# The last five column chunks of an input projection, computed by seven block products of 4 matmuls in place of 16 full ones

## Chip, cores and metric

The kernel runs on one core of a Trainium2 chip. The metric is the device time of one execution in microseconds (us), lower is better. Before the change three runs took 1416.8, 1419.84 and 1420.33 us, a median of 1419.84 us.

## What is computed

Two layers of a hybrid backbone for two groups of 128 tokens (a context group and a latent group), D_MODEL 1024, all in float32. Cut to the part that the change touches, a layer is:

```python
h  = x * (1 + scale1) + shift1                      # 2 groups x 128 tokens x 1024
(aq, ak, av, ao, gates, bq, bk, bv, cf_f, cf_b, cq, ci, cg,
 ga, gb, gc) = split(h @ w_in_l + b_in_l)           # w_in_l: 1024 x 9232
a_out, b_out, c_out = mlstm(...), attention(...), hgrn2(...)
y = (sigmoid(ga) * (a_out @ w_branch[0]) + sigmoid(gb) * (b_out @ w_branch[1])
     + sigmoid(gc) * (c_out @ w_branch[2])) @ w_out
x = layer_norm(ALPHA * x + gate1 * y)
y = hier_moe(x * (1 + scale2) + shift2)             # 16 experts
x = layer_norm(ALPHA * x + gate2 * y)
```

`ga`, `gb` and `gc` are 1024 wide each: they are the last six blocks of 512 columns of the projection. Keys, values and final states are outputs too.

## The kernel before

**Tiling.** The projection of a layer is cut into 18 chunks (`N_IN`) of 512 columns. A chunk's weights are one slot of 128 partitions x 4096 floats (2 MB), streamed into a ring of three slots (`ring`) by the SyncE queue; a slot is asked for again as soon as its last reader has counted up `slot_used`. The activations lie turned in `hT` (features on partitions, 8 blocks of 128, by 256 tokens). For a chunk TensorE runs, for each of the two groups of tokens, 8 matmuls with a 128x128 block of `hT` as stationary operand and 512 weight columns moving (line 974; a float32 matmul leaves two records in the trace, so 16 matmuls are "x32"). Three early chunks are computed turned, with 256 moving columns (line 970). VectorE reads each group's 512 sums from its own PSUM bank (`PJ`, `PJ + 1`), adds the bias and writes `ch` (line 1662).

**Order.** The program is written by hand in "quarters": quarter `q` of a layer belongs to chunk `q // 4`; quarters 0 and 1 of a chunk are group 0, quarters 2 and 3 group 1. Each engine's loop over quarters first emits the rounds of the recurrences that are set to that quarter (`in_order`), and then its share of the chunk. The rounds (`H_ROUNDS`, `T_ROUNDS`) are chains that go from TensorE to the other engines and back: each round waits on TensorE until the round before it is done on all engines. In the last chunks of a layer the rounds of the neighbourhood attention are left. Those of one head parity of the latent group are: scores (`na_scores`, quarters 58 and 63, lines 878 and 881 on TensorE, lines 1606 to 1617 on VectorE, with one ScalarE Exp, line 1289, in the middle), probabilities (`na_probs`, quarters 60 and 65, line 727) and output (`na_out`, quarters 62 and 67, lines 890 and 892).

**Between the chunks.** After some chunks a slot with modulation weights is multiplied by 8 narrow matmuls of 512 columns (`mod_products`, line 744, bank `MODS`), which VectorE adds to `rows` (line 1668): in layer 0 after chunks 13, 14, 15 and 16 among others, in layer 1 after chunk 14 only, of the last five.

**Sigmoids.** Chunks 12 to 17 are `ga`, `gb` and `gc`. Their sigmoid is ScalarE Exp (line 1334), GpSimd +1 and minimum (line 1970, `sig_plus`), ScalarE Ln and Exp (lines 1336 and 1337), for one group of one chunk at a time, in the one buffer `sig`.

**End of the stage.** At quarter 68 (`TURN_AT`) the branches' outputs are transposed (line 911) and the modulation rows summed (lines 961 and 777); after the last chunk the branch products follow (line 998), which wait for `rows_copied`, `mod_ready` and `br_ready`. The loads of the norm's weights and the gates into `hbuf` stand in the SyncE queue after the load of the first branch slot (`norm_and_gates`).

## Time and profile before

| what | value |
|---|---|
| median of three runs | 1419.84 us |
| profiled execution, its span (the rows and sums below are of this one) | 1419.9 us |
| TensorE (PE) busy | 1355.3 us, 95% |
| weight loads (PEld) busy | 744.6 us, 52% |
| VectorE (DVE) busy | 507.2 us, 36% |
| ScalarE (ACT) busy | 222.8 us, 16% |
| GpSimd (POOL) busy | 149.8 us, 11% |
| DMA | 376.28 MB, mean 265 GB/s |
| input projection, branches and output projection of layer 0 and of layer 1 | end near 460 and 1140 us |

Busy time is the time in which at least one instruction of the engine ran; TensorE's matmuls overlap, and their ends are modelled. Which engine sets the time has to be read stage by stage: the span holds two layers, each with an input projection (chunks 0 to 17), branch and output projections, and 16 experts.

### The profile page before, as it was taken

How to read it: one execution, taken by the hardware profiler on the slowest of the kernel's cores; microseconds unless marked ns; L12 is line 12 of the kernel's file. 1: busy time of each engine (PE TensorE's matmuls, PEld its weight loads, DVE VectorE, ACT ScalarE, POOL GpSimd, SP SyncE). 2: the span in 40 equal slices, each digit the busy share in tenths (PEclk: the TensorE clock that was granted, in tenths of full speed). 3: DMA queues.
4: the chain of work that ended last, by engine and by line, in shares of the span. 5: the costliest groups of instructions: out<-in, count | busy, mean ns of one | idle time of the engine just before them, and what ended most of it. 6: DMA issues, size and time to landing. Idle time of an engine off the chain costs nothing. (4 is left out here: it accounts for less than half of the span.)

```text
span 1419.9 us, 17185 instructions
## 1 busy us (share of the span) xinstructions
PE 1355.3 (95%) x6796; PEld 744.6 (52%) x6796; DVE 507.2 (36%) x972; ACT 222.8 (16%) x430; POOL 149.8 (11%) x131
## 2 busy tenths in 40 slices
PE   5999999999999999999989999999999999999994
PEld 2675545444545555555537655554554465555552
DVE  1224454433134422332252345452313343232324
ACT  0011221222201111111110213112230111011110
POOL 0002441022100000000001044402120000000000
PEclk9899999999999999999999999999999999999998
DMA  9655644556455899999993526343426729999993
GB/s 382 244 209 193 235 192 156 237 192 252 163 202 229 332 393 399 399 413 414 411 369 140 216 110 230 134 147 135 192 85 265 296 74 393 398 414 393 413 412 137
DMA packets 44488, 376.28 MB, mean 265 GB/s; under 512 B 13066, under 2 KB 17290, under 8 KB 21644
## 3 DMA queue, kind: packets, MB, share of 16 engines
q1 hardware_dynamic: 36000, 372.18, 65.3%
q10 hardware_dynamic: 8428, 3.29, 0.9%
q8 instruction: 40, 0.66, 0.2%
q14 instruction: 20, 0.16, 0.0%
HBM read 371.11 MB, written 4.33 MB: 264 GB/s over the span
## 5 line engine op out<-in xcount | busy, mean ns | idle before, releaser
L974 PE MATMUL psum<-ring,hT 128*128 128x512 f32 x960 | 431.5, 598 | 5.6 <-ACT hT L1187 2.2
L974 PEld LDWEIGHTS psum<-ring,hT 128*128 128x128 f32 x960 | 177.4, 191 | 206.0 <-issue 197.8
L1094 PE MATMUL psum<-ring,tbuf 128*64 128x256 f32 x1920 | 216.0, 380 | 3.5 <-DMA ring<-in_stream 3.5
L1094 PEld LDWEIGHTS psum<-ring,tbuf 128*64 128x64 f32 x1920 | 136.0, 137 | 96.8 <-issue 20.3
L1133 PE MATMUL psum<-ring,tbuf 128*64 128x512 f32 x512 | 116.9, 598 | 1.9 <-ACT tbuf L1382 1.9
L1812 DVE TENSOR_SCALAR tbuf<-tbuf 128x256 f32<-128x256 f32 x32 | 9.4, 294 | 243.8 <-ACT tbuf L1372 243.8
L1662 DVE TENSOR_TENSOR ch<-psum,bias_ring 128x512 f32<-128x512 f32 x56 | 38.6, 690 | 140.9 <-PE psum L974 140.9
L970 PE MATMUL psum<-hT,ring 128*128 128x256 f32 x384 | 85.4, 380 | 0.0
L998 PE MATMUL psum<-ring,tbuf 128*128 128x512 f32 x192 | 82.9, 593 | 0.0
L970 PEld LDWEIGHTS psum<-hT,ring 128*128 128x128 f32 x384 | 72.5, 190 | 13.0 <-issue 3.7
L1970 POOL TENSOR_SCALAR ldata<-ldata 128x512 f32<-128x512 f32 x24 | 46.1, 1920 | 253.2 <-ACT ldata L1334 241.5
L1078 PE MATMUL psum<-tbuf,ch 128*128 128x128 f32 x512 | 65.0, 281 | 6.8 <-DVE tbuf L1807 5.0
L1133 PEld LDWEIGHTS psum<-ring,tbuf 128*64 128x64 f32 x512 | 34.1, 136 | 69.8 <-issue 58.5
L1101 PE MATMUL psum<-tbuf 64*128 64x512 f32 x256 | 67.4, 626 | 1.4 <-ACTq L540 0.7
L1078 PEld LDWEIGHTS psum<-tbuf,ch 128*128 128x128 f32 x512 | 59.4, 191 | 15.5 <-issue 8.5
L998 PEld LDWEIGHTS psum<-ring,tbuf 128*128 128x128 f32 x192 | 36.3, 190 | 45.1 <-issue 45.0
L1012 PE MATMUL psum<-ring,hT 128*128 128x512 f32 x128 | 55.8, 594 | 1.4 <-ACT hT L1344 1.4
L1813 DVE RECIPROCAL tbuf<-tbuf 128x256 f32<-128x256 f32 x32 | 56.1, 1753 | 1.1
L355 POOL TENSOR_TENSOR hbuf<-hbuf 128x512 f32<-128x512 f32 x28 | 46.0, 1644 | 90.5 <-PE psum L797 90.5
L797 PEld LDWEIGHTS psum<-hbuf 128*128 128x128 f32 x256 | 34.4, 192 | 17.6 <-issue 12.9
L1385 ACT ACTIVATE tbuf<-psum 128x512 f32<-128x512 f32 x32 | 19.1, 597 | 154.7 <-PE psum L1133 154.7
L1807 DVE COPY tbuf<-psum 128x512 f32<-128x512 f32 x32 | 22.1, 691 | 51.4 <-PE psum L1078 51.4
(279 smaller groups left out, 1161.5 us busy)
## 6 DMA issues: line engine op xcount, KB each, us to landing
ring<-in_stream SPq DMA_DIRECT2D x154, 2048.0 KB, 9.7
ch<-in_stream SPq DMA_DIRECT2D x8, 2048.0 KB, 13.7
bias_ring<-in_b_in SPq DMA_DIRECT2D x30, 256.0 KB, 8.2
ldata<-in_ldata SPq DMA_DIRECT2D x2, 2329.0 KB, 19.8
tbuf<-in_stream SPq DMA_DIRECT2D x2, 2048.0 KB, 14.4
hbuf<-in_ln SPq DMA_DIRECT2D x4, 1024.0 KB, 10.7
hbuf<-in_stream SPq DMA_DIRECT2D x1, 2048.0 KB, 8.6
hbuf<-row_mem SPq DMA_DIRECT2D x2, 1024.0 KB, 4.7
```

Of the source, the lines that this page charges most:

```text
L355: return engine.tensor_tensor(v, v, other.unsqueeze(3).to_broadcast([P, 2, W // (2 * half), half]), ALU.mult)
L970: mm = pe.matmul(psum[:, PJ + g, part * G * P:(part + 1) * G * P], w[:, k, (2 * g + part) * P:(2 * g + part + 1) * P], hT[:, k, :], start= ...
L974: mm = pe.matmul(bank(PJ + g), hT[:, k, g * P:(g + 1) * P], w[:, k, :], start=(k == 0), stop=(k == KT - 1))
L998: mm = pe.matmul(bank(BR_BANK[g] + hf), brT[:, b % 2, k, g * P:(g + 1) * P], w[:, k, hf * W:(hf + 1) * W], start=(k == 0), stop=(k == BT - 1))
L1012: mm = pe.matmul(bank(2 * hf + g), hT[:, k, g * P:(g + 1) * P], w[:, k, :], start=(k == 0), stop=(k == KT - 1))
L1078: mm = pe.matmul(psum[:, at, j * P:(j + 1) * P], h2tok[:, g, (4 * part + j) * P:(4 * part + j + 1) * P], e_pick[:, g, :], start=(g == 0), ...
L1094: mm = pe.matmul(psum[halves_of[hf], UP[j], 0:FE // 2], xgT[:, k, halves_of[i]], w_up[:, k, hf * (FE // 2):(hf + 1) * (FE // 2)], start=(k ...
L1101: pe.matmul(bank(Y_MOE[g][hf]), e_selT[i][halves_of[hf], g, :], e_out[halves_of[hf], :], start=opens, stop=closes)\
L1133: mm = pe.matmul(psum[halves_of[hf], OUT, :], ehidT[:, (k % 2) * P + (k // 2) * CAP:(k % 2) * P + (k // 2) * CAP + CAP], w_down[:, k, hf * ...
L1662: ins = tt(ch[:, g, c if c < 12 else GATE_BUF[c - 12], :], bank(PJ + g), bias_ring[:, c % RING, :], ALU.add)
L1813: mlink(dve.reciprocal(esig, esig))
L1970: pool.tensor_scalar(sig, sig, 1.0, LN_MAX, ALU.add, ALU.min).then_inc(sig_plus, 1)
```

## The change

The chunks 13 to 17 (`FAST`) of each layer are computed by Strassen's scheme in its form with seven block products. The product of 256 tokens x 1024 features with 1024 x 512 weights is taken as 2x2 blocks: A11 to A22 are 128 tokens x 512 features, B11 to B22 are 512 x 256 weights. A product is 4 matmuls with 256 moving columns. There are four sums of blocks of A (`S1` to `S4`, once per layer, VectorE, `a_sums`), and four sums of quarters of the weights for each chunk: `T1`, `T2`, `T4` on VectorE (in `fast_part`), `T3` on GpSimd (`weight_sum`), each 128 x 1024 elements. They lie in `hbuf`, which is free then. The products use banks 0, 1 and 5; two of them are added on top of another in PSUM. VectorE reads the banks with ten instructions of 256 columns for each chunk instead of two of 512.

```diff
+FAST = list(range(13, N_IN))
+A_SUMS_AT = 4 * FAST[0] - 3
+FAST_ORDER = [["A11 B11", "S4 B22"], ["S1 T1", "S2 T2"], ["A12 B21", "S3 T3"], ["A22 T4"]]
+        BANK_OF = {"A11 B11": PJ + 1, "A12 B21": PJ + 1, "S1 T1": PJ, "A22 T4": PJ, "S4 B22": 5, "S2 T2": 5, "S3 T3": 5}
+        FAST_MODS = PJ + 1
 (sync)
-                    if (kind, c) == ("branch", 0):
+                    if (kind, c) == ("branch", 2):
+                        sp.wait_ge(product_filled, filled(l, FAST[-1], "A22 T4"))
...
                         norm_and_gates(l, 0)
 (tensor)
+                def product(c, p):
+                    first, before = c == FAST[0], max(c - 1, FAST[0])
+                    if p == "A11 B11":
+                        slot(l, "in", l, c)
+                        pe.wait_ge(*((proj_read, proj(l, c - 1, 1)) if first else (product_read, evacuated(l, before, "A12 B21"))))
+                        if not first and before in MODS_AFTER[l]:
+                            pe.wait_ge(rows_added, added(*MODS_AFTER[l][before]))
+                    if p == "S4 B22":
+                        pe.wait_ge(a_summed, l + 1)
...
+                            pe.wait_ge(product_read, evacuated(l, before, "S3 T3"))
+                    if p == "S1 T1":
+                        pe.wait_ge(proj_read, proj(l, c - 1, 1))
+                        pe.wait_ge(b_summed, fast(l, c) * 3 + 1)
+                    if p == "S2 T2":
+                        pe.wait_ge(product_read, evacuated(l, c, "S4 B22"))
+                        pe.wait_ge(b_summed, fast(l, c) * 3 + 2)
+                    if p == "A12 B21":
+                        pe.wait_ge(product_read, evacuated(l, c, "A11 B11"))
+                        pe.wait_ge(b_summed, fast(l, c) * 3 + 3)
+                        pe.wait_ge(b_summed_pool, fast(l, c) + 1)
+                    if p == "S3 T3":
+                        pe.wait_ge(product_read, evacuated(l, c, "S2 T2"))
+                    if p == "A22 T4":
+                        pe.wait_ge(product_read, evacuated(l, c, "S1 T1"))
+                    a, b = p.split()
+                    on_top = p in ("A12 B21", "S3 T3")
+                    for k in range(4):
+                        mm = pe.matmul(psum[:, BANK_OF[p], 0:HALF], a_block(a)[:, k, :], b_block(l, c, b)[:, k, :],
+                                       start=(k == 0 and not on_top), stop=(k == 3), skip_group_check=on_top)
+                def fast_mod(c):
...
+                    pe.wait_ge(product_read, evacuated(l, c, "A12 B21"))
...
+                    if c in FAST:
+                        for p in FAST_ORDER[q % 4]:
+                            if q % 4 == 3 and c in MODS_AFTER[l]:
+                                fast_mod(c)
+                            product(c, p)
+                        continue
 (vector)
+                def fast_part(c, part):
+                    if part == 0:
+                        if c > FAST[0]:
+                            dve.wait_ge(product_filled, filled(l, c - 1, "A22 T4"))
+                        chunk_arrived(dve, l, c)
+                        tt(b_sum["T1"], block("B12"), block("B11"), ALU.subtract).then_inc(b_summed, 1)
+                        tt(b_sum["T2"], block("B22"), b_sum["T1"], ALU.subtract).then_inc(b_summed, 1)
...
+                        tt(out(2, 1), p_("A11 B11"), bias[0], ALU.add)
+                        tt(out(2, 2), p_("A11 B11"), bias[1], ALU.add).then_inc(product_read, 1)
+                        tt(out(1, 2), out(2, 2), p_("S4 B22"), ALU.add).then_inc(product_read, 1)
+                    if part == 1:
+                        tt(b_sum["T4"], b_sum["T2"], block("B21"), ALU.subtract).then_inc(b_summed, 1)
+                        tt(out(2, 2), out(2, 2), p_("S1 T1"), ALU.add)
+                        tt(out(1, 2), out(1, 2), p_("S1 T1"), ALU.add).then_inc(product_read, 1)
+                        tt(out(1, 2), out(1, 2), p_("S2 T2"), ALU.add).then_inc(product_read, 1)
+                    if part == 2:
+                        tt(out(1, 1), p_("A12 B21"), bias[0], ALU.add).then_inc(product_read, 1)
+                        tt(out(2, 2), out(2, 2), p_("S3 T3"), ALU.add)
+                        tt(out(2, 1), out(2, 1), p_("S3 T3"), ALU.add).then_inc(product_read, 1)
+                    if part == 3:
...
+                            tt(rows[:, lm, :], rows[:, lm, :], bank(FAST_MODS), ALU.add).then_inc(rows_added, 1)
+                        tt(out(2, 1), out(2, 1), p_("A22 T4"), ALU.subtract).then_inc(proj_read, 1)
 (gpsimd)
+                def weight_sum(c):
+                    if c == FAST[0]:
+                        pool.wait_ge(a_summed, l + 1)
+                    else:
+                        pool.wait_ge(product_filled, filled(l, c - 1, "S3 T3"))
+                    chunk_arrived(pool, l, c)
+                    tt(b_sum["T3"], b_block(l, c, "B22"), b_block(l, c, "B12"), ALU.subtract).then_inc(b_summed_pool, 1)
```

The sigmoid of a chunk's group 0 now stands in the chunk's last quarter and that of group 1 in the second quarter of the next chunk, on ScalarE and GpSimd; the transposes of the second branch are moved by two quarters.

How the change moves instructions, at the two places that the prediction speaks of. First TensorE, layer 0, from the scores round of quarter 58 to the probabilities of quarter 60. Before (878 and 881 are the scores, 974 the chunk's matmuls, 744 the modulation, 727 the transposes of the probabilities):

```order
L878 MATMUL psum<-tbuf 128x128 x4
L881 MATMUL psum<-tbuf 128x128 x4
L974 MATMUL psum<-ring,hT 128x512 x8
L744 MATMUL psum<-ring,scZ 32x512 x8
L727 MATMUL psum<-const,tbuf 128x128 x8
L974 MATMUL psum<-ring,hT 128x512 x8
```

And with the change (936 and 939 are the scores, 1036 the block products, 802 the modulation, 785 the transposes):

```order
L936 MATMUL psum<-tbuf 128x128 x4
L939 MATMUL psum<-tbuf 128x128 x4
L1036 MATMUL psum<-ring,hT 128x256 x4
L1036 MATMUL psum<-hbuf 128x256 x4
L802 MATMUL psum<-ring,scZ 32x512 x8
L1036 MATMUL psum<-hbuf,hT 128x256 x4
L785 MATMUL psum<-const,tbuf 128x128 x8
```

Between the scores and the modulation stand now two block products (A12 B21 and S3 T3), where 8 matmuls of twice the columns stood. Second VectorE, the same place. Before (1606 to 1617 are the scores round, 1662 the read of a group's bank, 1668 the addition to `rows`, 1619 the copy of the probabilities):

```order
L1613 TENSOR_REDUCE sm<-tbuf 128x4
L1615 TENSOR_REDUCE sm<-tbuf 128x4
L1616 TENSOR_TENSOR sm<-sm 128x4
L1617 RECIPROCAL sm<-sm 128x4
L1662 TENSOR_TENSOR ch<-psum,bias_ring 128x512
L1668 TENSOR_TENSOR rows<-rows,psum 128x512
L1619 COPY tbuf<-psum 128x512
```

And with the change (1728 to 1732 are the end of the scores round, 1784 the read of A12 B21, 1795 the addition to `rows`, 1762, 1764 and 1774 the sums T1, T2 and T4, the rows with 128x256 the other reads of block products):

```order
L1728 TENSOR_REDUCE sm<-tbuf 128x4
L1730 TENSOR_REDUCE sm<-tbuf 128x4
L1731 TENSOR_TENSOR sm<-sm 128x4
L1732 RECIPROCAL sm<-sm 128x4
L1784 TENSOR_TENSOR ch<-psum,bias_ring 128x256
L1788 TENSOR_TENSOR ch<-ch,psum 128x256
L1789 TENSOR_TENSOR ch<-ch,psum 128x256
L1795 TENSOR_TENSOR rows<-rows,psum 128x512
L1798 TENSOR_TENSOR ch<-ch,psum 128x256
L1734 COPY tbuf<-psum 128x512
L1762 TENSOR_TENSOR hbuf<-ring 128x1024
L1764 TENSOR_TENSOR hbuf<-ring,hbuf 128x1024
```

The read of a block product stands right behind the whole scores round, and the sums of the next chunk's weights behind all reads of this one.

## Rows read from the trace of the kernel before

**Rows 1.** Page, part 1: busy time of each engine over the whole span.

```profile
PE 1355.3 (95%) x6796; PEld 744.6 (52%) x6796; DVE 507.2 (36%) x972; ACT 222.8 (16%) x430; POOL 149.8 (11%) x131
```

**Rows 2.** Windows, chunks 13 to 17: stretch, length, busy by engine, PEclk, DMA share, GB/s.

```profile
313.59:380.94 67.35, 67.35 (x267) 33.82 (x267) 19.98 (x37) 18.32 (x27) 13.11 (x7) 1.00 0.48 186
1000.07:1062.47 62.40, 62.40 (x227) 32.26 (x227) 18.39 (x34) 18.33 (x27) 13.10 (x7) 1.00 0.33 127
```

**Rows 3.** Timeline of PE: unbroken stretches at 256 and 512 columns (start us, us).

```profile
785.58 13.98 PE L970 MATMUL psum<-hT,ring 128*128 128x256 f32 x64
799.40 13.90 PE L974 MATMUL psum<-ring,hT 128*128 128x512 f32 x32
...
1047.74 13.98 PE L974 MATMUL psum<-ring,hT 128*128 128x512 f32 x32
1061.56 1.04 PE L911 MATMUL psum<-const,ch 128*128 128x128 f32 x8
```

**Rows 4.** Lines by form, DVE and POOL: busy us, mean ns, idle before.

```profile
L1821 DVE TENSOR_TENSOR tbuf<-tbuf,psum 128x256 f32<-128x256 f32 x32 | 13.5, 421 | 36.9 <-PE psum L1094 36.9
L1486 DVE SCALAR_TENSOR_TENSOR hbuf<-hbuf 128x1024 f32<-128x1024 f32 x4 | 4.9, 1225 | 0.1
L1951 POOL TENSOR_TENSOR spare<-ch,const 128x512 f32<-128x512 f32 x4 | 5.1, 1268 | 11.2 <-PE psum L865 11.0
L1970 POOL TENSOR_SCALAR ldata<-ldata 128x512 f32<-128x512 f32 x24 | 46.1, 1920 | 253.2 <-ACT ldata L1334 241.5 <-PE psum L727 11.7
```

**Rows 5.** Timeline of DVE: the scores round of chunk 14, layer 0.

```profile
313.69 0.69 DVE L1606 TENSOR_REDUCE sm<-psum 128x4 f32<-128x512 f32 x1 [1.29 <-PE psum L881]
...
318.44 0.69 DVE L1613 TENSOR_REDUCE sm<-tbuf 128x4 f32<-128x512 f32 x1 [1.21 <-ACT tbuf L1289]
...
320.08 0.18 DVE L1617 RECIPROCAL sm<-sm 128x4 f32<-128x4 f32 x1
320.76 0.69 DVE L1662 TENSOR_TENSOR ch<-psum,bias_ring 128x512 f32<-128x512 f32 x1 [0.51 <-PE psum L974]
```

**Rows 6.** Timeline of PE over the same stretch.

```profile
313.59 7.13 PE L974 MATMUL psum<-ring,hT 128*128 128x512 f32 x16
320.65 1.93 PE L744 MATMUL psum<-ring,scZ 128*32 128x512 f32 x16
```

**Rows 7.** Timelines where POOL and DVE instructions overlap, layer 0.

```profile
114.23 1.34 POOL L1898 TENSOR_TENSOR hbuf<-hbuf 128x512 f32<-128x512 f32 x1 [32.28 <-ACT hbuf L1211]
114.36 1.75 DVE L1489 TENSOR_TENSOR hbuf<-hbuf 128x512 f32<-128x512 f32 x1
...
168.62 1.27 POOL L1951 TENSOR_TENSOR spare<-ch,const 128x512 f32<-128x512 f32 x1 [5.50 <-PE psum L865]
168.86 1.05 DVE L1504 TENSOR_SCALAR sm<-sm 128x4 f32<-128x4 f32 x1
```

**Rows 8.** Timeline of PE: four stretches, the idle time before them in brackets.

```profile
22.95 7.10 PE L974 MATMUL psum<-ring,hT 128*128 128x512 f32 x16 [1.74 <-DMA ring<-in_stream]
...
41.84 9.98 PE L974 MATMUL psum<-ring,hT 128*128 128x512 f32 x16 [2.18 <-ACT hT L1187]
...
724.59 6.43 PE L744 MATMUL psum<-ch,scZ 128*32 128x512 f32 x32 [3.19 <-PEq L540]
...
743.44 7.11 PE L974 MATMUL psum<-ring,hT 128*128 128x512 f32 x16 [1.71 <-DVE hT L1451]
```

**Rows 9.** Windows behind two of those idle times, columns as in rows 2.

```profile
42.00:47.00 5.00, 5.00 (x6) 2.03 (x7) 0.00 (x0) 0.00 (x0) 0.00 (x0) 0.50 0.69 191
724.00:730.00 6.00, 5.41 (x28) 1.59 (x32) 5.68 (x9) 0.41 (x2) 0.00 (x0) 0.50 0.88 309
730.00:733.00 3.00, 3.00 (x19) 1.50 (x12) 1.55 (x6) 0.85 (x3) 0.00 (x0) 0.96 0.98 411
```

**Rows 10.** Timeline of SP's queue: the second of the loads that the change moves.

```profile
383.08 0.33 SPq L605 DMA_DIRECT2D hbuf<-row_mem  x1
```

**Rows 11.** Timeline of DVE: the first reader of both.

```profile
432.48 0.69 DVE L1706 TENSOR_TENSOR hbuf<-psum,hbuf 128x512 f32<-128x512 f32 x1 [8.64 <-PE psum L1012]
```

More of the change, by code:

```diff
@@ L239, in build @@
         y = hbuf[:, 0:4 * W].rearrange("p (g n) -> p g n", g=G)
+        a_sum = dict(zip(("S1", "S2", "S3", "S4"), (hbuf[:, i * W:(i + 1) * W].rearrange("p (k t) -> p k t", k=4) for i in range(4))))
+        b_sum = dict(zip(("T1", "T2", "T3", "T4"), (hbuf[:, (4 + 2 * i) * W:(6 + 2 * i) * W].rearrange("p (k n) -> p k n", k=4) for i in range(4))))
         lnb = [hbuf[:, 4 * W:8 * W].rearrange("p (a n) -> p a n", a=2), hbuf[:, 0:4 * W].rearrange("p (a n) -> p a n", a=2)]
@@ L498, in proj, with fast, filled, evacuated @@
             return l * (2 * N_IN) + (2 * RING + 2 * c + g + 1)
+        def fast(l, c):
+            return l * len(FAST) + FAST.index(c)
+        def filled(l, c, p):
+            return fast(l, c) * len(DONE) + DONE[p]
+        def evacuated(l, c, p):
+            return fast(l, c) * len(READ) + READ[p]
+        def a_block(name):
+            if name in a_sum:
+                return a_sum[name]
+            i, j = int(name[1]) - 1, int(name[2]) - 1
+            return hT[:, 4 * j:4 * j + 4, i * P:(i + 1) * P]
+        def b_block(l, c, name):
+            if name in b_sum:
+                return b_sum[name]
+            i, j = int(name[1]) - 1, int(name[2]) - 1
+            w = ring[:, (RING_BASE[l] + AT[l]["in", l, c]) % RING, :].rearrange("p (k n) -> p k n", k=KT)
+            return w[:, 4 * i:4 * i + 4, j * HALF:(j + 1) * HALF]
+        def chunk_arrived(eng, l, c):
+            i = AT[l]["in", l, c]
+            eng.wait_ge(slot_loaded[(RING_BASE[l] + i) % RING], arrived(l, i))
+        def sigmoid_at(q):
+            if q % 2 == 0 or q < 4 * 12:
+                return []
+            n = (q - 4 * 12) // 2
+            if 12 + n // 2 < FAST[0]:
+                return [(12 + n // 2, n % 2)]
+            return [(12 + m // 2, m % 2) for m in ([n - 1] if n % 2 else ([n - 1] if 12 + (n - 1) // 2 >= FAST[0] else []))]
         def added(l, m):
@@ L1327, in _ @@
                                       ch[:, 0, c, :].rearrange("p (h n) -> p h n", h=NAH)).then_inc(kv_stored, 16)
-                    if q % 2 and c >= 12:
-                        act.wait_ge(proj_read, proj(l, c, g))
-                        if (l, c, g) == (1, 12, 0):
-                            act.wait_ge(rows_added, MOD_ADDS.index((1, LAYER_MODS)) + 1)
-                        v = ch[:, g, GATE_BUF[c - 12], :]
-                        act.activation(sig, v, ACT.Exp, scale=-1.0).then_inc(sig_exp, 1)
-                        act.wait_ge(sig_plus, l * 12 + ((c - 12) * 2 + g + 1))
-                        link(act.activation(sig, sig, ACT.Ln))
-                        link(act.activation(v, sig, ACT.Exp, scale=-1.0))
+                    for sc, sg in sigmoid_at(q):
+                        sigmoid(sc, sg)
+                sigmoid(N_IN - 1, 1)
                 act.sem_inc(gates_ready, 1)
@@ L1647, in _ @@
                     c, g = q // 4, (q // 2) % 2
-                    if q % 2:
+                    if q == A_SUMS_AT:
+                        a_sums()
+                    if c in FAST:
+                        fast_part(c, q % 4)
+                    elif q % 2:
                         if g:
@@ L1964, in _ @@
                         rotate()
-                    c, g = q // 4, (q // 2) % 2
-                    if q % 2 and c >= 12:
-                        pool.wait_ge(sig_exp, l * 12 + ((c - 12) * 2 + g + 1))
-                        pool.sem_inc(pool_tick, 1)
-                        pool.tensor_scalar(sig, sig, 1.0, LN_MAX, ALU.add, ALU.min).then_inc(sig_plus, 1)
+                    if q // 4 in FAST and q % 4 == 0:
+                        weight_sum(q // 4)
+                    for sc, sg in sigmoid_at(q):
+                        sigmoid_plus(sc, sg)
+                sigmoid_plus(N_IN - 1, 1)
                 if l + 1 < DEPTH:
```

77 lines of the change are left out of this document (71 added, 6 removed).

## Prediction

> **What bounds the kernel now.** I read the engines' share of the span first: TensorE is busy 95%, VectorE 36%, ScalarE 16%, GpSimd 11% [rows 1]. A mean over stages decides nothing, so the second view is the windows over the chunks that change. There TensorE is busy for every microsecond (67.35 of 67.35 in layer 0, 62.40 of 62.40 in layer 1) at full clock, VectorE for some 19 us, and the DMA share is 0.48 and 0.33 [rows 2]. So here the time is the sum of TensorE's matmuls, weights arrive early, and each microsecond taken off TensorE is one off the kernel, if nobody makes TensorE wait. The third view, the timelines of VectorE and TensorE side by side, shows how close the waits are.
>
> **The gain.** Three unbroken stretches give the price of a column. 32 matmuls of 256 columns start at 785.58 and the next work at 799.40: 13.82 us, 0.432 each. A whole chunk of 512 columns runs from 1047.74 to 1061.56, 13.82 us for 16 matmuls [rows 3]. Half the columns cost half the time, nothing more. A chunk in seven products is 28 x 0.432 = 12.09 us, one product 1.73 us. The gain is 1.73 us a chunk, **17.3 us for ten**. That is the whole of it; the DMAs of the weights are the same.
>
> **What VectorE gets.** A read of 256 columns from PSUM costs 0.42 us, a sum over 1024 columns 1.23 us [rows 4]: ten reads and three sums are 7.9 us a chunk, against 12.1 us of products. On average that fits. But before the change the two banks gave VectorE the time of half a chunk, 6.9 us, for each read; now product n+2 mostly waits for the read of product n. Take the end of a chunk's last product as zero. VectorE reads it (to 0.5), makes T1 (to 1.7) and T2 (to 3.0), then does three reads (to 4.3). TensorE wants T1 at 3.5 and the third read at 5.2. The slack is 0.9 us. The sums of A (four of 512 columns, 2.8 us) stand in chunk 12, which still has two banks and 6.9 us of cover: nothing; without that cover they would cost up to 2.8 us a layer.
>
> **The scores rounds.** Twice in the last five chunks of each layer VectorE has a scores round in its queue. The one of chunk 14 runs from 313.69 to 320.26 [rows 5], 6.6 us, with a ScalarE Exp in the middle for which the queue stands. Before, TensorE worked on its next 8 matmuls from 313.59 to 320.65 [rows 6], and the reads behind the round were only then due. Now only two products, 3.5 us, stand between the scores and the modulation, and the modulation waits for the read behind the round: 6.6 + 0.5 - 3.5 = 3.6 us of standstill. In chunk 15 of layer 0 the next chunk waits for the round and the addition to the rows (6.6 + 0.8), with modulation and one product (1.9 + 1.7) as cover: 3.8 us. In layer 1 there is no modulation; TensorE gets three products further (5.2), waits 1.5 for the round, and then 1.5 more for T1, T2 and their reads, which are late: 3.0. So 7.4 in layer 0 and 6.6 in layer 1, and I add 1 us a layer for waits under 1 us (the first fast chunk's T1 stands behind a round, too). **Cost 16 us**, ends 13 and 19.
>
> **Two engines, one way into SBUF.** GpSimd's instruction at 114.23 took 1.34 us; VectorE's sum of two SBUF operands, started at 114.36, took 1.75 instead of 0.69, that is it began when GpSimd's ended. Even a sum over 4 columns took 1.05 beside a GpSimd instruction of 1.27 [rows 7]. T1, T2 and T4 have two SBUF operands. GpSimd's part of a chunk is T3, about 2.4 us (an estimate: twice the 1.27 us of its sum over 512 columns, less one start), and two +1 of 1.92 us [rows 4]. Follow the start of a chunk: the +1 of group 0 ends near -0.2, T3 runs from there to 2.2. T1 waits and runs 2.2 to 3.4; the +1 of group 1, ready at 1.4, is next, to 5.3; T2 follows to 6.6, the three reads to 7.8. TensorE wanted them at 5.2: 2.6 us of standstill. The starts of chunks 14 to 17 are exposed; at 17 the transposes and row sums (about 3 us) cover it, and the modulation before 14, and in part before 16, does so in layer 0. I count 1.5 times in layer 0, 3 times in layer 1: 4.5 x 2.6, **12 us**. No row shows a VectorE sum beside the +1 itself, so the lower end is 0; if the pairs queue at every start it is 18. I take 12 because the nearest row, of the same form on VectorE, shows the full wait. The Trainium skill's page "SBUF — State Buffer", section "Who interferes with whom", says that a VectorE instruction with two SBUF inputs contends with a GpSimd instruction that reads SBUF, and that the later one fully blocks. The +1 reads SBUF, so by that rule the sum is the 12 us above. By the trace's pairs alone (sum beside sum) half of the holds would fall away, and the sum be some 6 us.
>
> **The clock.** After an idle time of 3.19 us TensorE's granted clock was 0.50 for 6 us, that is 1.2 GHz, and 32 narrow records took 6.43 us where 16 take 1.93 at full clock [rows 6, 8, 9]: 2.6 us lost. After 2.18 us it was 0.50 again, and 16 records took 9.98 instead of 7.10: 2.9 us lost. After 1.71 us it stayed at 2.4 GHz (7.11) [rows 8, 9]. The four scores rounds give standstills of 3.0 to 5 us each, above the longest idle time for which I have the fall. 4 x 2.75 is 11; but products at half clock take 3.5 us and let VectorE catch up, which hides part of a port wait. **9 us**, ends 0 and 15.
>
> **Moved loads.** The norm's weights and the gates are now asked for behind all three branch loads and the last product. The second of them went out at 383.08 [rows 10] because it waits for the summed rows, and is first read at 432.48 [rows 11]: 49 us of cover. Nothing; if the cover were gone, one transfer of 1 MB. The branch weights are asked for earlier. The last sigmoid ends as far behind the last product as before. Nothing.
>
> **Sum.** -17.3 + 16 + 12 + 9 = +19.7 us on the profiled 1419.9, which is the median of the runs too (1419.84): **1440 us**, +1.4%. This case's own range is 1427 to 1451. A difference under 0.3%, 4.3 us, can't be told from none.
>
> **Rivals.**
> *No hold at the port, or only now and then.* The +1 never met a two-operand sum before, and GpSimd may let T1 pass. Then -17.3 + 16 + 9 = +7.7: 1428. For it: only pairs of sums are in the rows. Against it: both pairs there show the wait.
> *The stalls alone.* Neither the port nor the clock bites: -17.3 + 16 = -1.3, 1418.6, no change. The clock stays up if the standstills come out under 2 us. Against it: three of the four are worked out from a round whose 6.6 us stand in the trace.
> *Faster.* VectorE keeps up: TensorE waits only at the first scores round of each layer, 2 x 3.6 = 7.2, because in the second the round starts earlier against TensorE's queue, and the port costs nothing. -17.3 + 7.2 = -10: 1410. The place is the read behind the scores round; the point from which it decides is 8.65 us of waits a layer, half the gain. For it: 7.9 us of VectorE work in 12.1. Against it: a round of 6.6 us is longer than the 3.5 us of products in front of its read, wherever it starts.
> *Worse.* All exposed starts queue and the clock falls behind the port's waits too: 16 + 18 + 15 - 17.3 = +32, 1452.
>
> **How the numbers follow.** Forecast 0.60, no port 0.20, stalls alone 0.09, faster 0.06, worse 0.05. The forecast is the likeliest case. From 1421 to 1452 I leave out the faster case, most of the unchanged one and a little above: under 2 in 10. Slower by over 0.3%: 0.60 + 0.20 + 0.05, less 0.01 for a mild port case near the bound, 0.84. Within 0.3%: 0.09. Faster: 0.07, with the edge of the unchanged case.
>
> **What would show it.** In the profile after: 280 matmuls of block products that take 0.432 us each where they are unbroken; TensorE idle in front of the modulation of chunk 14 by 3 to 4 us in both layers, released by VectorE; idle of 2 to 3 us in front of S2 T2, with T1 or T2 on VectorE lasting 2 to 3 us instead of 1.23 beside a GpSimd row; PEclk of 0.50 in windows behind these. Wrong on the port if all T1 and T2 last 1.23. Wrong on the clock if PEclk stays 1.00 through the last five chunks. Wrong altogether if TensorE's idle time in them is under 8 us a layer.

## Result and profile after the change

The changed kernel takes 1427.88 us (median of four runs, 1426.12 to 1430.81) against 1418.32 us for the kernel before in the same series. The ratio is 1.007 with a 95% interval of 1.0056 to 1.0085: **slower by 9.6 us**, about half of the 20 us forecast. The profiled execution has a span of 1428.9 us, 9.0 above the one before.

The page of the changed kernel, part 1, answers to [rows 1]:

```profile
PE 1348.2 (94%) x7036; PEld 793.6 (56%) x7036; DVE 586.1 (41%) x1090; ACT 222.2 (16%) x430; POOL 179.2 (13%) x141
```

TensorE has 7.1 us less to do, by records, and the kernel lost time all the same. VectorE's busy time is 79 us longer, GpSimd's 29; time in which an instruction is held counts as busy.

Windows of the changed kernel over the end of the projection in layers 0 and 1, from a scores round in chunk 12 (in layer 1 from just before it) to the branch products (columns as in rows 2):

```profile
281.06:383.97 102.91, 94.15 (x500) 73.23 (x499) 64.34 (x105) 25.09 (x39) 33.17 (x15) 0.97 0.55 205
971.00:1072.54 101.54, 90.93 (x451) 72.78 (x452) 63.72 (x101) 25.73 (x40) 34.45 (x15) 0.95 0.40 143
```

Where TensorE was busy all the time at full clock [rows 2], it is now idle for nearly a tenth, at a mean clock of 0.97 and 0.95. The end of layer 0's projection is 3.0 us later than before (383.97 against 380.94), the same scores round at the end of layer 1's projection starts 2.5 us later (971.78 against 969.28), the end of layer 1's projection is 10.1 us later (1072.54 against 1062.47), and the whole 9.0. So the time is lost between chunk 12 and the branch products of each layer, and the stages behind each give back 0.5 to 1 us.

TensorE's timeline in the changed kernel: the first row is an unbroken stretch, the others are the rows of the changed chunks with an idle time, which stands in brackets with its releaser (one more, at 979.14, is like the one at 285.63, with 0.88).

```profile
289.60 3.62 PE L1036 MATMUL psum<-hbuf 128*128 128x256 f32 x16
...
285.63 1.96 PE L1036 MATMUL psum<-ring,hT 128*128 128x256 f32 x8 [0.88 <-DVE ch L1839]
318.55 3.52 PE L802 MATMUL psum<-ring,scZ 128*32 128x512 f32 x16 [3.36 <-issue]
328.70 1.97 PE L1036 MATMUL psum<-hbuf 128*128 128x256 f32 x8 [0.39 <-DVE hbuf L1762]
331.28 1.99 PE L1036 MATMUL psum<-hbuf 128*128 128x256 f32 x8 [0.61 <-DVE ch L1771]
347.79 2.47 PE L1036 MATMUL psum<-ring,hT 128*128 128x256 f32 x8 [3.53 <-DVE rows L1795]
999.80 1.99 PE L1036 MATMUL psum<-hbuf 128*128 128x256 f32 x8 [0.51 <-DVE ch L1771]
1010.78 3.19 PE L802 MATMUL psum<-ring,scZ 128*32 128x512 f32 x16 [3.36 <-issue]
1020.99 1.97 PE L1036 MATMUL psum<-hbuf 128*128 128x256 f32 x8 [0.38 <-DVE hbuf L1762]
1023.56 1.99 PE L1036 MATMUL psum<-hbuf 128*128 128x256 f32 x8 [0.61 <-DVE ch L1771]
1039.45 1.06 PE L785 MATMUL psum<-const,tbuf 128*128 128x128 f32 x8 [1.29 <-issue]
1040.95 1.97 PE L1036 MATMUL psum<-hbuf 128*128 128x256 f32 x8 [0.44 <-DVE hbuf L1762]
1045.28 3.67 PE L1036 MATMUL psum<-hbuf 128*128 128x256 f32 x8 [2.36 <-DVE ch L1771]
```

Line 1036 is a product, 802 the modulation, 785 the transposes of the probabilities; 1762 is T1, 1771 the read of S4 B22 that frees the bank of S2 T2, 1795 the addition to the rows. The first row starts at 289.60 and the next work at 293.05: two products in 3.45 us, 1.73 each as forecast. The idle times add up to 8.8 us in layer 0 (0.88, 3.36, 0.39, 0.61, 3.53) and 9.8 in layer 1 (0.88, 0.51, 3.36, 0.38, 0.61, 1.29, 0.44, 2.36): 18.6 us. "issue" at the modulation hides a releaser: line 802 waits for the read of A12 B21, the first one behind VectorE's scores round. An idle chain that ends in "issue" still has a semaphore in front of it, and the program tells which.

VectorE's timeline around chunk 14 of layer 0, changed kernel: the scores round (first and last row of it), and the read that the modulation waits for.

```profile
311.57 0.69 DVE L1721 TENSOR_REDUCE sm<-psum 128x4 f32<-128x512 f32 x1 [1.23 <-PE psum L939]
...
317.96 0.18 DVE L1732 RECIPROCAL sm<-sm 128x4 f32<-128x4 f32 x1
318.05 0.39 DVE L1784 TENSOR_TENSOR ch<-psum,bias_ring 128x256 f32<-128x256 f32 x1
```

It is the walk of the prediction: the round lasts 6.6 us from 311.57, the read ends at 318.44, the modulation starts at 318.55. The two products in front started at 311.47, and at 1.73 us each their successor was due at 314.92. From start to start the standstill is 3.6 us, as forecast; the bracket says 3.36 because it counts from the modelled end of the last product.

3-us windows of the changed kernel behind three of the long standstills; the third column from the right is the granted clock:

```profile
320.00:323.00 3.00, 3.00 (x17) 1.13 (x10) 0.69 (x1) 1.26 (x2) 1.28 (x1) 0.70 0.03 14
350.00:353.00 3.00, 3.00 (x9) 2.32 (x8) 2.97 (x4) 0.00 (x0) 0.16 (x1) 0.58 0.01 5
1046.00:1049.00 3.00, 3.00 (x8) 2.36 (x8) 1.61 (x3) 1.18 (x2) 0.00 (x0) 0.53 0.00 0
```

The clock fell to 1.2 GHz four times behind standstills of the changed chunks. 16 narrow records of the modulation took 3.52 us where they took 1.93 at full clock [rows 6], a product 3.67 where it takes 1.99. Each fall costs 1.6 to 1.7 us, **6.7 us for the four**. A fifth fall is in a place where I expected nothing; the section on the prediction has it.

### The profile page after: what moved, and what is told of

Same layout as the page of the kernel before. It is cut to its first block and busy times, and to the rows that moved or that the text cites. A ratio compares the mean times of both kernels' runs of the same rounds, so it can differ in the third digit from the quotient of the medians.

```text
span 1428.9 us, 17893 instructions
## 1 busy us (share of the span) xinstructions
PE 1348.2 (94%) x7036; PEld 793.6 (56%) x7036; DVE 586.1 (41%) x1090; ACT 222.2 (16%) x430; POOL 179.2 (13%) x141
## 5 line engine op out<-in xcount | busy, mean ns | idle before, releaser
L1083 PE MATMUL psum<-ring,hT 128*128 128x512 f32 x640 | 289.4, 600 | 4.3 <-ACT hT L1296 2.2
L1083 PEld LDWEIGHTS psum<-ring,hT 128*128 128x128 f32 x640 | 118.5, 192 | 137.7 <-issue 131.3
L2142 POOL TENSOR_SCALAR ldata<-ldata 128x512 f32<-128x512 f32 x24 | 51.1, 2131 | 228.6 <-ACT ldata L1423 228.6
L1036 PE MATMUL psum<-hbuf 128*128 128x256 f32 x240 | 58.0, 390 | 5.3 <-DVE ch L1771 4.1
L1121 PE MATMUL psum<-ring,hT 128*128 128x512 f32 x128 | 55.8, 594 | 1.4 <-ACT hT L1459 1.4
L1839 DVE TENSOR_TENSOR ch<-psum,bias_ring 128x512 f32<-128x512 f32 x36 | 24.9, 691 | 70.2 <-PE psum L1083 70.1
L1036 PEld LDWEIGHTS psum<-hbuf 128*128 128x128 f32 x240 | 45.5, 194 | 13.9 <-DVE ch L1771 5.7
## 6 DMA issues: line engine op xcount, KB each, us to landing
tbuf<-in_stream SPq DMA_DIRECT2D x2, 2048.0 KB, 14.2
```

The lines of the kernel that those rows point to most:

```text
L1036: mm = pe.matmul(psum[:, BANK_OF[p], 0:HALF], a_block(a)[:, k, :], b_block(l, c, b)[:, k, :], start=(k == 0 and not on_top), stop=(k == 3) ...
L1083: mm = pe.matmul(bank(PJ + g), hT[:, k, g * P:(g + 1) * P], w[:, k, :], start=(k == 0), stop=(k == KT - 1))
L1121: mm = pe.matmul(bank(2 * hf + g), hT[:, k, g * P:(g + 1) * P], w[:, k, :], start=(k == 0), stop=(k == KT - 1))
L2142: pool.tensor_scalar(sig, sig, 1.0, LN_MAX, ALU.add, ALU.min).then_inc(sig_plus, 1)
```

## Experiments

All are edits of the changed kernel, compared with the kernel before on the same chip. The changed kernel itself was timed only in the series of the result, so what is said against it goes by the two ratios to the kernel before. "Idle" is TensorE's idle time in the changed chunks, added up as above. Two theories stand: **the forecast**, in which the hold at the port costs 12 us of standstill, and **the trace's theory**, in which it costs 4 to 5, because only T3 holds VectorE's sums.

### T3 left out

```diff
 b_block(l, c, name)
+            if name == "T3":
+                name = "T1"
 weight_sum(c)
-                    tt(b_sum["T3"], b_block(l, c, "B22"), b_block(l, c, "B12"), ALU.subtract).then_inc(b_summed_pool, 1)
+                    pool.sem_inc(b_summed_pool, 1)
```

> GpSimd's sum T3 is left out in all ten fast chunks (S3 is multiplied by T1 in its place, so those outputs are not the reference's); nothing else is changed. The forecast's port term (12 us, of which the holds of T1 behind T3 are the larger part) expects 8 us or more less than the changed kernel's 1428. What the trace of the changed kernel shows (T1 of 2.5 and 3.0 us beside T3, but only some 4 us of TensorE idle behind them) expects 3 to 5 us less, 1423 to 1425, and T1 of 1.23 us at every chunk start. If T3's holds are all covered, no difference.

Measured: 1422.58 us, 1.0028 [1.0016, 1.0039]. That is 5 to 6 us less than the changed kernel, not the 8 or more of the forecast, and a little more than the 3 to 5 of the trace's theory, which had not counted a fall of the clock. The idle times of 0.39, 0.61, 0.51, 0.38, 0.61 and 2.36 are gone, but for one of 0.32; idle is 14.0 us, 4.6 less, and there is one fall of the clock less. The port costs TensorE 4.6 us of standstill and one fall, not 12 us of standstill.

### The +1 left out in chunks 13 to 17

```diff
-                    pool.tensor_scalar(sig, sig, 1.0, LN_MAX, ALU.add, ALU.min).then_inc(sig_plus, 1)
+                    if c in FAST:
+                        pool.sem_inc(sig_plus, 1)
+                    else:
+                        pool.tensor_scalar(sig, sig, 1.0, LN_MAX, ALU.add, ALU.min).then_inc(sig_plus, 1)
```

> GpSimd's +1 of the sigmoids is left out in chunks 13 to 17 (the gates come out wrong; ScalarE's three steps stay). If a running +1 holds VectorE's sums for its whole 1.92 us, as the forecast assumed, this takes 4 us or more off the changed kernel. If it holds them only at its start (the trace shows T4 at 1.21 us beside a +1), at most 1 us, 1427 to 1429.

Measured: 1429.64 us, 1.0091 [1.0066, 1.0116]: nothing won. The two waits of 0.61 in front of S2 T2 are 0.32 here, so the +1 costs 0.3 us at such a place; the 0.51 and the 2.36 are gone. It is not a clean experiment, though: with the +1 out of GpSimd's queue T3 starts earlier, and falls into VectorE's scores round. GpSimd, VectorE and TensorE of this kernel in chunk 15 of layer 0:

```profile
343.72 2.35 POOL L2154 TENSOR_TENSOR hbuf<-ring 128x1024 f32<-128x1024 f32 x1 [18.29 <-ACT ldata L1423]
344.35 1.73 DVE L1731 TENSOR_TENSOR sm<-sm 128x4 f32<-128x4 f32 x1
...
347.03 3.65 PE L1036 MATMUL psum<-ring,hT 128*128 128x256 f32 x8 [5.10 <-DVE rows L1795]
```

A sum over 4 columns waits until T3 ends (346.07) and makes the round 1.6 us longer; TensorE's standstill behind it is 5.10 us instead of 3.53, and in layer 1, where the same sum takes 1.74 us beside T3, it is 2.87 instead of 1.29. That is what the +1 had kept away by standing in front of T3: in the changed kernel it ran from 345.92, and T3 started at 347.81, behind the round.

### The long standstills filled with matmuls

```diff
 product("A11 B11")
+                        if c == 16 and l == 0:
+                            hold_clock(3, bank(PP))
 product("S2 T2")
+                        if c == 16 and l == 1:
+                            hold_clock(2, bank(PP))
 fast_mod(c)
+                    if c == 14:
+                        hold_clock(3, bank(PP))
```

`hold_clock(n)` is n matmuls of 512 columns whose result nobody reads; they stand in front of the wait.

> Three matmuls of 512 columns on constants (2.6 us) are put in front of each of the waits of 3.4 to 3.5 us behind the scores rounds, and two before the 2.4 us one in layer 1; they use a bank that nobody reads. If the falls of the granted clock behind these waits cost what the trace shows (1.6 to 1.8 us each, four of them), PEclk stays 1.00 and the time falls by 6 to 7 us, to 1421 to 1422. If slow products only fill time in which TensorE would wait for VectorE anyway, under 3 us. If the filling itself delays, it gets slower.

Measured: 1422.07 us, 1.0028 [1.0015, 1.004], about 6 us less than the changed kernel. Windows of this kernel:

```profile
281.00:384.00 103.00, 99.44 (x520) 75.58 (x519) 64.34 (x105) 26.24 (x41) 34.76 (x16) 1.00 0.58 218
971.00:1073.00 102.00, 96.49 (x471) 74.47 (x470) 63.75 (x101) 27.42 (x42) 36.37 (x16) 1.00 0.46 174
```

The clock is 1.00 throughout, and the waits themselves are as they were: the 3.36 in front of the modulation is now 2.6 of matmuls and 0.74 idle. So the clock term is 6 us. Work that nobody needs, put where TensorE stands still, made the kernel faster.

### The modulation in a bank of its own

```diff
-        FAST_MODS = PJ + 1
+        FAST_MODS = PP
 product("A11 B11")
-                        if not first and before in MODS_AFTER[l]:
-                            pe.wait_ge(rows_added, added(*MODS_AFTER[l][before]))
 fast_mod(c)
-                    pe.wait_ge(product_read, evacuated(l, c, "A12 B21"))
```

Bank `PP` is free there. No wait on VectorE's reads is left in front of the modulation, and the next chunk's first product need not wait for the addition to the rows.

> The modulation behind a fast chunk writes bank 4 in place of bank 1, which the block products use, so its two waits (for the read of A12 B21, and of the next chunk for the addition to the rows) go. Theory 1, the standstill is a bank that is asked back too early: the idle times of 3.4, 3.5 and 3.4 us go, with three of four clock falls, 10 to 15 us less, 1413 to 1418, under the kernel before. Theory 2, VectorE is late whatever the bank, and the wait turns up at the next product or round: 4 us less or nothing, 1424 to 1428. I hold something between the two for likely, 7 to 10 us.

Measured: 1418.58 us, 1.0008 [0.9994, 1.0021], equal to the kernel before: about 9 us less than the changed kernel. The standstills of 3.36, 3.53 and 3.36 are gone, and are found again in part as what was late next: 1.47 in front of S2 T2 of chunk 15, 2.80 in front of S1 T1 of chunk 16, 1.46 in layer 1. Idle is 12.1 us and two falls of the clock are left. This shows the cause of the larger part of these standstills: a bank is asked back from VectorE two products after it was given (one product, behind the modulation), while a long round stands in front of its read. The rest, the waits that turned up in front of S1 T1 and S2 T2, is VectorE being late with other things.

### All banks spread

```diff
-        BANK_OF = {"A11 B11": PJ + 1, "A12 B21": PJ + 1, "S1 T1": PJ, "A22 T4": PJ, "S4 B22": 5, "S2 T2": 5, "S3 T3": 5}
-        FAST_MODS = PJ + 1
+        BANK_OF = {"A11 B11": PJ + 1, "A12 B21": PJ + 1, "S1 T1": PJ, "A22 T4": PJ, "S4 B22": 5, "S2 T2": PP, "S3 T3": PP}
+        FAST_MODS = EX
 product("S4 B22")
-                            pe.wait_ge(product_read, evacuated(l, before, "S3 T3"))
+                            pe.wait_ge(product_read, evacuated(l, before, "S4 B22"))
 product("S2 T2")
-                        pe.wait_ge(product_read, evacuated(l, c, "S4 B22"))
+                        if c > FAST[0]:
+                            pe.wait_ge(product_read, evacuated(l, c - 1, "S3 T3"))
```

The two waits around the modulation are taken out as above.

> Banks only: S2 T2 and S3 T3 go to bank 4, the modulation to bank 2, so S2 T2 no longer waits for the read of S4 B22, nor the modulation and the next chunk for VectorE's reads and additions. If asked-back banks are what the VectorE queue stands behind, the remaining idle times of the last run (1.5 us twice and 2.4 us at S2 T2) go as well: 12 to 15 us less than the changed kernel, 1413 to 1416, and 3 to 5 less than with the modulation's bank alone. If VectorE's sums T1 and T2 are late on their own, only 1 to 2 us less than that run, about 1417.

Measured: 1412.43 us, 0.996 [0.9948, 0.9973]: faster than the kernel before by about 6 us. S2 T2 no longer waits for a read of its own chunk. The largest idle time left is the wait for T1 itself, as the timeline of this kernel on GpSimd, VectorE and TensorE shows:

```profile
340.16 2.35 POOL L2149 TENSOR_TENSOR hbuf<-ring 128x1024 f32<-128x1024 f32 x1
340.23 0.63 ACT L1423 ACTIVATE ldata<-ldata 128x512 f32<-128x512 f32 x1 [2.15 <-POOL ldata L2140]
340.25 3.35 DVE L1760 TENSOR_TENSOR hbuf<-ring 128x1024 f32<-128x1024 f32 x1
...
343.74 5.38 PE L1035 MATMUL psum<-hbuf 128*128 128x256 f32 x16 [2.79 <-DVE hbuf L1760]
```

T1 is 0.09 us behind T3 and waits for all of it.

### T1 and T2 made a chunk earlier

```diff
+                def first_sums(c):
...
                     if part == 0:
-                        tt(b_sum["T1"], block("B12"), block("B11"), ALU.subtract).then_inc(b_summed, 1)
-                        tt(b_sum["T2"], block("B22"), b_sum["T1"], ALU.subtract).then_inc(b_summed, 1)
+                        if c == FAST[0]:
+                            first_sums(c)
...
                     if part == 1:
+                        if c > FAST[0]:
+                            dve.wait_ge(product_filled, filled(l, c - 1, "A22 T4"))
                         tt(b_sum["T4"], b_sum["T2"], block("B21"), ALU.subtract).then_inc(b_summed, 1)
...
+                        if c < FAST[-1]:
+                            first_sums(c + 1)
```

The banks are those of the changed kernel. VectorE makes T1 and T2 of chunk c + 1 at the end of part 1 of chunk c, ahead of the scores round.

> Order only: VectorE makes T1 and T2 of the next chunk at the end of this chunk's second part, before the scores rounds, in place of at the start of the next chunk; banks as in the changed kernel. The port theory (T1 held behind T3 at the chunk's start) expects the idle times at S1 T1 and S2 T2 (about 5 us in all) to go: 3 to 5 us less, about 1424. The standstill of 3.4 us in front of the modulation stays, since its bank and its read stay. If lateness of T1 and T2 costs nothing by itself, the time stays at 1428.

Measured: 1424.58 us, 1.0033 [1.0019, 1.0047], 4 to 5 us less than the changed kernel. All idle times in front of S1 T1 and S2 T2 are gone, but the sums push the scores round back, and the two standstills in front of the modulation are 4.17 us instead of 3.36. Idle is 14.9 us.

### Banks and early sums together

Both edits.

> Both: the banks of the run banks and the order of the run early_t, T3 still on GpSimd. If TensorE's waits in the five chunks are banks and late sums and nothing else, under 4 us of its 18.6 us of idle time stay, the clock never falls, and the time is 1403 to 1408, 0.7 to 1.1% under the kernel before. If the two edits only shift the same lateness, it is no better than the run banks.

Measured: **1406.42 us** (1403.98 to 1408.29), 0.9904 [0.9887, 0.9921]: 12.7 us faster than the kernel before by medians, 13.6 by the ratio, and some 23 us faster than the changed kernel by the two ratios. Windows of this kernel, and the rows of TensorE with an idle time in the changed chunks (in layer 1 the first, of 0.88, comes back too):

```profile
281.00:384.00 103.00, 102.04 (x527) 77.30 (x526) 59.83 (x108) 27.45 (x42) 34.89 (x16) 1.00 0.62 236
965.00:1063.00 98.00, 95.75 (x472) 75.07 (x471) 56.83 (x101) 27.84 (x42) 34.89 (x16) 1.00 0.48 182
```

```profile
285.22 1.97 PE L1035 MATMUL psum<-ring,hT 128*128 128x256 f32 x8 [0.88 <-DVE ch L1845]
...
1019.87 1.06 PE L785 MATMUL psum<-const,tbuf 128*128 128x128 f32 x8 [1.29 <-issue]
```

Idle is 3.1 us, and the clock stays up in the changed chunks: -17.3 + 3.1 is -14.2, inside the measured interval (-16.0 to -11.2 us). The gain that was forecast is there, once nobody takes it back.

### T3 on VectorE, without and with these two edits

```diff
 fast_part, part 1
                         tt(b_sum["T4"], b_sum["T2"], block("B21"), ALU.subtract).then_inc(b_summed, 1)
+                        tt(b_sum["T3"], block("B22"), block("B12"), ALU.subtract).then_inc(b_summed_pool, 1)
 gpsimd
-                    if q // 4 in FAST and q % 4 == 0:
-                        weight_sum(q // 4)
```

> The changed kernel with T3 on VectorE behind T4, nothing else. It takes the same GpSimd sum away as the run no_t3 did, but keeps the result right and pays 1.23 us more on VectorE a chunk. If the 5 us that no_t3 gained were the holds of T1 and T2 behind T3, this gains 3 to 5 us over the changed kernel, 1423 to 1425, with T1 and T2 of at most 1.5 us. If VectorE's queue is what is short, it gains nothing.

Measured on the changed kernel's plan: 1423.96 us, 1.0034 [1.0019, 1.0048], 4 to 5 us less than the changed kernel. The port is out of it, with nothing left out of the computation. TensorE's rows at chunk 16 of layer 1 in this kernel:

```profile
1034.95 1.07 PE L785 MATMUL psum<-const,tbuf 128*128 128x128 f32 x8 [1.30 <-issue]
1036.45 1.96 PE L1036 MATMUL psum<-hbuf 128*128 128x256 f32 x8 [0.44 <-DVE hbuf L1762]
1038.74 1.99 PE L1036 MATMUL psum<-hbuf 128*128 128x256 f32 x8 [0.33 <-DVE ch L1771]
1041.70 1.97 PE L1036 MATMUL psum<-ring,hT 128*128 128x256 f32 x8 [0.96 <-DVE hbuf L1775]
```

Without the port the second scores round of layer 1 costs 1.30 + 0.44 + 0.33 + 0.96 = 3.0 us, which is the figure of the prediction. Idle is 15.0 us.

> As the run best_pool, with T3 on VectorE too (behind T4), so that GpSimd has no weight sums and no port conflict with them is left. If the port still costs something in best_pool, this is 1 to 3 us faster than it; if VectorE's own queue is what is short, the 1.23 us more a chunk make it 1 to 3 us slower than best_pool. I hold the second for likelier.

Measured with both edits: 1407.22 us, 0.9918 [0.9901, 0.9934], not to be told from 1406.42. Where the sums have slack, the engine that makes T3 does not matter; idle is 4.8 us, since VectorE's queue is a little longer.

### Banks spread and T3 left out

> The run banks with T3 left out (S3 is multiplied by T1 in its place, so those outputs are not the reference's). In the run banks 2.8 us of idle time stood before S1 T1 in layer 0 and 1.3, 0.4 and 0.7 in layer 1, with one clock fall each. If these are T1 and T2 held behind T3, they shrink to under 2 us in all and the time falls by 3 to 6 us, to 1407 to 1409, near the run best_pool without its order. If they are VectorE's late start behind the scores round, under 1 us is gained.

Measured: 1408.78 us, 0.9917 [0.9899, 0.9934], about 6 us less than with the banks alone. The idle time of 2.79 in front of S1 T1 is 0.66 here, and both of the clock's falls are gone: with spread banks, most of what was left was T3's hold. One of the two falls is not explained by it: it came at 1024 us behind idle times of 1.29 and 0.44 us, and this kernel has the same two (1.30 and 0.44) without a fall.

### The runs side by side

us; gain -17.3 in all; "falls" are falls of the clock in the changed chunks at 1.7 us each; measured is the ratio's difference from 1 by 1419, with its interval.

| kernel | idle | falls | sum | measured |
|---|---|---|---|---|
| changed kernel | 18.6 | 4 | +8.1 | +9.9 (7.9 to 12.1) |
| the +1 left out | 18.3 | 4 | +7.8 | +12.9 (9.4 to 16.5) |
| filled | 18.6 with the filling | 0 | +1.3 | +4.0 (2.1 to 5.7) |
| T3 left out | 14.0 | 3 | +1.8 | +4.0 (2.3 to 5.5) |
| T3 on VectorE | 15.0 | 3 | +2.8 | +4.8 (2.7 to 6.8) |
| early sums | 14.9 | 3 | +2.7 | +4.7 (2.7 to 6.7) |
| modulation's own bank | 12.1 | 2 | -1.8 | +1.1 (-0.9 to 3.0) |
| banks spread | 7.9 | 2 | -6.0 | -5.7 (-7.4 to -3.8) |
| banks spread, no T3 | 4.9 | 0 | -12.4 | -11.8 (-14.3 to -9.4) |
| banks and early sums | 3.1 | 0 | -14.2 | -13.6 (-16.0 to -11.2) |
| the same, T3 on VectorE | 4.8 | 0 | -12.5 | -11.6 (-14.0 to -9.4) |

The sums go nearly in the order of the measured values. All lie under them, by 0.3 to 5 us, seven of them by 1.8 us or more, and four lie under the interval. Three things are missing. First, a stop costs more than its bracket. In the rows of the changed kernel above, the product at 328.70 lasts 1.97 us up to its modelled end, and then come 0.61 idle; from its start to the next it is 2.58 us, where an unbroken product takes 1.73. That is 0.85 us lost, 0.24 more than the bracket, and the changed kernel has 13 such stops, the kernel with banks and early sums 3. Second, and the other way, the kernel before had an idle time of 0.62 us (with its own 0.24) in each layer there, in front of transposes, and it is gone in the changed kernel, 1.7 us in all:

```profile
297.79 1.09 PE L727 MATMUL psum<-const,ch 128*128 128x128 f32 x8 [0.62 <-ACTq L1293]
...
986.32 1.09 PE L727 MATMUL psum<-const,ch 128*128 128x128 f32 x8 [0.62 <-ACTq L1293]
```

Third, chunk 12 of layer 1 waits 0.6 us longer in all eleven, which the next section shows. Together this adds 13 x 0.24 - 1.7 + 0.6 = 2.0 us to the changed kernel's +8.1, an estimate of +10.1 against +9.9 measured. Worked out in the same way, ten of the eleven come to lie in their intervals, most of them in the lower half. The kernel without the +1 stays just under its own (+9.3, from 9.4): idle times and falls are those of one execution, which for it was the fastest of four (1427.21 us, median 1429.64) at a mean clock of 0.985, where two of the others have 0.983.

## Why the prediction was half right

**Direction and causes: right.** The kernel is slower, by standstills in front of a matmul that waits for VectorE and by the clock behind them.

**The gain, -17.3: right.** 1.73 us a product in the trace. The best kernel measures -13.6 with 3.1 us idle, so 16.7 us (14.3 to 19.1) of gain.

**The scores rounds, 16: right.** By the brackets it is a little high; from start to start the first standstill is the forecast 3.6. Layer 0 has 3.36 and 3.53 for 3.6 and 3.8, layer 1 has 3.36 for 3.6, and 3.0 for 3.0 where the port is out of it. With the two waits of 0.88 at the first product of chunk 13 (the "1 us a layer") the term is 15.0 with T3 on VectorE and 14.0 without T3. I gave those 0.88 to T1 behind a round; they are the wait for the read of chunk 12.

**The port, 12: wrong, 3.6 to 4.6.** This is the step that failed. The walk said "the +1 of group 1 is next, to 5.3; T2 follows": one hold by T3 and then a second, whole one by the +1. The trace shows the first and not the second. GpSimd and VectorE of the changed kernel, chunk 15 and (last two rows) chunk 14 of layer 0:

```profile
325.11 2.36 POOL L2151 TENSOR_TENSOR hbuf<-ring 128x1024 f32<-128x1024 f32 x1 [3.83 <-PE psum L785]
325.50 3.05 DVE L1762 TENSOR_TENSOR hbuf<-ring 128x1024 f32<-128x1024 f32 x1
...
327.43 2.90 POOL L2142 TENSOR_SCALAR ldata<-ldata 128x512 f32<-128x512 f32 x1
328.59 1.51 DVE L1764 TENSOR_TENSOR hbuf<-ring,hbuf 128x1024 f32<-128x1024 f32 x1
...
307.04 1.92 POOL L2142 TENSOR_SCALAR ldata<-ldata 128x512 f32<-128x512 f32 x1 [3.01 <-ACT ldata L1423]
...
308.01 1.21 DVE L1774 TENSOR_TENSOR hbuf<-hbuf,ring 128x1024 f32<-128x1024 f32 x1
```

T1 at 325.50 takes 3.05 us: T3 ends at 327.47, and T1 1.08 later. The +1 at 327.43 is itself held by T1 (2.90 for 1.92, so it works from 328.4), and T2, issued at 328.59, takes 1.51 instead of 1.22: it lost 0.3 us to the +1, not 1.9. T4 at 308.01 runs beside a running +1 (307.04 to 308.96) for all but its last 0.26 us, in its bare 1.21 us. The Trainium skill's page "SBUF — State Buffer", section "Who interferes with whom", has the later instruction fully blocked; the trace agrees for T1 behind T3, and does not agree for T2 and T4 beside the +1. The prediction had both sums worked out: 12 by the rule, "some 6" by the trace's own pairs. The rows of before supported only the 6, and I took the 12 for a pair that no row showed. (In the second pair of rows 7 VectorE's instruction isn't a sum at all, but one with a single SBUF tensor; GpSimd's is a two-operand sum in both.) With 0.3 us in the place of the 1.9, the same walk gives 2.6 - 1.6 = 1.0 us of standstill for a chunk start, and 0.39 + 0.61 and 0.38 + 0.61 us are what chunk 15 shows in the two layers. So the hold by T3 and the slack of 0.9 us were right, and one term of the walk was wrong. The starts differ: 0.51 us at chunk 14 of layer 1, and 2.36 at its chunk 16, behind the scores round. The upper end of 18 doesn't follow from the count in the prediction either: eight exposed starts of 2.6 us are 21, the six without chunk 17 are 16.

**The clock, 9: 6.7 in the changed chunks, 5.9 by the filled kernel.** The count of four came true, but in part by luck: the fourth fall, at 1045.28, needed T3's hold. The scores round of chunk 16 in layer 1 alone, 3.0 us in four pieces, had no fall behind it in the kernel with T3 on VectorE. The price was wrong. I took 2.75 a fall from low stretches of 6 us [rows 8, 9]; these last some 3.4 us (3.52 for the modulation's records at 318.55) and cost 1.7.

**What the walk missed: the sums of A, "nothing".** VectorE, ScalarE and TensorE of the changed kernel in chunk 12 of layer 1: the last of the four sums, the read of the chunk's first group, the end of that group's sigmoid, and the scores and the matmuls behind them.

```profile
966.25 0.68 DVE L1748 TENSOR_TENSOR hbuf<-hT,hbuf 128x512 f32<-128x512 f32 x1
966.85 0.68 DVE L1839 TENSOR_TENSOR ch<-psum,bias_ring 128x512 f32<-128x512 f32 x1
...
971.03 0.63 ACT L1426 ACTIVATE ch<-ldata 128x512 f32<-128x512 f32 x1
971.78 1.16 PE L936 MATMUL psum<-tbuf 64*128 64x128 f32 x8 [1.23 <-ACTq L1402]
...
972.87 5.40 PE L1083 MATMUL psum<-ring,hT 128*128 128x512 f32 x8
```

The read has its bank in time, so TensorE's next matmuls are not late, as I argued. But the sigmoid hangs on the read, ScalarE's queue on the sigmoid, and the scores on ScalarE's queue. The same wait was 0.64 us before the change:

```profile
969.28 1.16 PE L878 MATMUL psum<-tbuf 64*128 64x128 f32 x8 [0.64 <-ACTq L1293]
```

It is 1.23 now, and in this execution the clock fell behind it: 8 records took 5.40 us, 3.70 in other kernels of the series. That is 0.6 us in layer 1 always and 2.3 where the clock falls (it did in four of the eleven profiled kernels). The other three executions of the changed kernel have a mean clock of 0.985 to 0.986, the profiled one 0.984, so this fall probably isn't in all of them. This is read from the traces; no kernel was run without the sums of A. With it the profiled execution adds up to -17.3 + 18.6 + 6.7 + 2.3 = +10.3, against +9.0 measured between the profiled executions; the stops' 0.24 us and the idle time of 0.62 that went, from above, add 1.4, and the stages in front and behind give back the rest.

**The moved loads, nothing: right.** No idle time of TensorE between chunk 17 and the branches in either layer.

**The rivals.** The time is that of "no hold at the port" (1428), by luck. Its mechanism is not what happened: there is a hold, by T3 alone, and the clock and the A sums have other sizes than in its sum. The chance of 0.60 for a full double hold was too high for a price of which the nearest row showed half.

In sum, 20 forecast against 10: of the gap 7.4 to 8.4 is the port, 2.3 to 3 the clock, 1 to 2 the scores rounds as the brackets count them, and the sums of A give 0.6 to 2.3 back.

## What to carry to other kernels

A scheme that saves multiplications for the price of more results makes each of them shorter, and so shortens the cover behind which the reading engine used to do its long rounds. Here the arithmetic saved 17.3 us exactly as computed, and some 27 (17.3 and the 9.6 lost) were given back, the larger part by seven results in three banks and by operand sums behind the rounds. When work on the busiest engine gets finer, ask for each PSUM bank how many products pass between giving it away and asking it back, and compare that with the longest round in the reader's queue; then put operand sums ahead of that round and not behind it. Against the kernel before, the banks alone brought -5.7 us and the early sums alone left +4.7; both together gave -13.6.

The long standstills cost 1.7 us more each through the clock: in the changed chunks of the eleven kernels all 20 idle times of 2.36 us or more were followed by a fall. Where one can't be removed, matmuls that nobody reads are worth putting there.

## What the hardware showed that was not expected

- A hold between GpSimd and VectorE depends on GpSimd's instruction. The sum of two SBUF operands (T3, 2.36 us) holds VectorE's two-operand sums for its whole length, even one over 4 columns (1.73 us). The +1, with one operand, holds them only near its own start. Beside a +1 that has just begun they lose 0.3 to 0.4 us (T2: 1.51 for 1.22; T3 on VectorE: 1.63, below), issued 0.37 us behind its start they lose 0.1 (1.32, in the kernel with spread banks and no T3), and 0.7 us or more behind it nothing (1.21). All of these fit a hold of the first 0.47 us of the +1, an estimate: where it was itself held, its start is taken as its end less 1.92. The spans of GpSimd in a profile are rough, so whether the +1 lets go early or its record is long stays open. The kernel with T3 on VectorE, chunk 14 of layer 0:

```profile
307.00 2.70 POOL L2143 TENSOR_SCALAR ldata<-ldata 128x512 f32<-128x512 f32 x1 [5.35 <-ACT ldata L1423]
307.84 1.63 DVE L1775 TENSOR_TENSOR hbuf<-ring 128x1024 f32<-128x1024 f32 x1
```

- The hold works the other way too: T3 takes 2.93 us and the +1 2.90 when they are issued during a VectorE sum, where their bare times are 2.36 and 1.92.
- Leaving an instruction out can cost time: without the +1, T3 moved into the scores round, and one standstill grew from 3.53 to 5.10 us.
- The same idle time of 1.23 us in front of the same matmuls was followed by a fall of the clock in four kernels and by none in seven. So the length of the last idle time doesn't decide alone; what does has not been found.
